# A decoder step on one core: for token blocks 2 and 3 of the last stage, first expert's weighted rows and residual computed on Pool instead of VectorE

## The reference

```python
combine = jnp.sum(jax.nn.one_hot(expert, N_EXPERTS) * w_top[..., None], axis=1)   # two weights per token
for g in range(N_GROUPS):
    act = jax.nn.silu(a) * u * combine[:, sl, None]
    out = out + jnp.einsum('nef,efd->nd', act, w_ed[sl])
x = x + moe(...)                      # the residual
y = _rmsnorm(x, norm_final)           # x * rsqrt(mean(x * x) + 1e-6) * g, the output
```

## Time and profile before

| what | us |
|---|---|
| median of 3 runs | 789.47 (789.15 to 790.32) |
| the profiled execution | 787.27 |
| its span, first to last instruction | 785.1 |
| outside the span | 2.2 |
| TensorE busy | 727.7 |
| VectorE busy | 345.0 |
| ScalarE busy | 245.2 |
| Pool busy | 87.4 |

### The profile page before, as it was taken

The page is one execution under the profiler, slowest core; times in us unless marked ns, Lnnn a source line. Parts: engine busy times, 40 slices in busy tenths (PEclk is TensorE's granted clock), DMA queues, the critical chain, the costliest instruction groups (busy, mean ns, idle before and its releaser), DMA issues.

```text
span 785.1 us, 12498 instructions
## 1 busy us (share of the span) xinstructions
PE 727.7 (93%) x5154; PEld 537.6 (68%) x5154; DVE 345.0 (44%) x648; ACT 245.2 (31%) x495; POOL 87.4 (11%) x143
## 2 busy tenths in 40 slices
PE   4999999999999999999999999988999987877775
PEld 3898997778999999888999987874444332322221
DVE  6653349654565435444255533581222321111228
ACT  6333474554544442334122223321111111001013
POOL 2404000000000100100000001221131211111100
PEclk9999999999999999999999999999999999999998
DMA  8732111114122630722344469898999999999993
GB/s 318 234 109 63 55 54 54 55 54 108 54 59 84 229 142 28 269 81 81 108 149 148 162 201 387 332 336 321 418 417 417 418 418 418 419 417 418 420 388 155
DMA packets 83368, 176.64 MB, mean 225 GB/s; under 512 B 7919, under 2 KB 42063, under 8 KB 83296
## 3 DMA queue, kind: packets, MB, share of 16 engines
q1 hardware_dynamic: 72736, 148.51, 50.8%
q0 software_dynamic: 10576, 27.33, 9.4%
HBM read 161.68 MB, written 22.68 MB: 235 GB/s over the span
## 4 chain that ended last, share of the span: by engine, by line
PE 70%; SPq 14%; DVE 7%; DMA 4%; issue 3%; ACT 3%; ACTq 0%; POOLq 0%; DVEq 0%
PE bank L810 45%; SPq L587 11%; PE bank L1273 7%; PE bank L1290 4%; SPq L593 3%; DMA expert_down<-in_w_exp_down 2%; DVE w_split L1694 2%; ACT w_split L1362 1%; PE bank L830 1%; PE bank L1240 1%; PE bank L1095 1%; PE bank L1101 1%; DVE s_state L1998 1%; PE bank L1046 1%; PE bank L1056 1%
## 5 line engine op out<-in xcount | busy, mean ns | idle before, releaser
L810 PE MATMUL bank<-hT_split,w_split 128*128 128x272 f32 x1152 | 154.1, 292 | 0.0
L810 PEld LDWEIGHTS bank<-hT_split,w_split 128*128 128x128 f32 x1152 | 147.3, 188 | 2.1 <-issue 0.9
L1273 PE MATMUL bank<-expert_gate_up,gatheredT 128*64 128x512 f32 x512 | 116.5, 602 | 18.2 <-DMA expert_gate_up<-in_w_exp_up 16.0
L810 PE MATMUL bank<-w_split,hT_split 128*128 128x512 f32 (+1 forms) x576 | 130.1, 380 | 0.4 <-DVE w_split L1694 0.4
L810 PEld LDWEIGHTS bank<-w_split,hT_split 128*128 128x128 f32 x576 | 100.1, 188 | 22.9 <-issue 3.3
L1694 DVE TENSOR_TENSOR w_split<-w_raw,w_split 128x2048 fp32r<-128x2048 f32 (+1 forms) x35 | 75.9, 2168 | 83.3 <-ACT w_split L1362 83.3
L1273 PEld LDWEIGHTS bank<-expert_gate_up,gatheredT 128*64 128x64 f32 x512 | 39.6, 138 | 91.3 <-issue 67.0
L1362 ACT ACTIVATE w_split<-w_raw 128x2048 fp32r<-128x2048 f32 (+1 forms) x35 | 63.4, 1812 | 42.0 <-PE bank L810 17.5
L1290 PE MATMUL bank<-expert_down,expert_actT 128*64 128x512 f32 x256 | 58.5, 597 | 12.6 <-DMA expert_down<-in_w_exp_down 7.5
L2273 DVE TENSOR_TENSOR expert_act<-expert_silu,bank 128x256 f32<-128x256 f32 x16 | 6.7, 421 | 116.2 <-ACT expert_silu L1635 116.2
L810 PE MATMUL bank<-gla_outT_split,w_split 128*128 128x272 f32 x384 | 49.4, 288 | 0.0
(11 more groups left out here) (405 smaller groups left out, 862.6 us busy)
## 6 DMA issues: line engine op xcount, KB each, us to landing
expert_gate_up<-in_w_exp_gate SPq DMA_DIRECT2D x64, 512.0 KB, 14.9
expert_gate_up<-in_w_exp_up SPq DMA_DIRECT2D x64, 512.0 KB, 15.4
expert_down<-in_w_exp_down SPq DMA_DIRECT2D x32, 1024.0 KB, 17.5
w_raw<-in_w_in SPq DMA_DIRECT2D x15, 1024.0 KB, 5.9
w_raw<-in_w_in SPq DMA_DIRECT2D x16, 512.0 KB, 4.6
s_state<-in_state_gla POOLq DMA_DIRECT2D x4, 1024.0 KB, 10.3
out_sample_gla_state<-s_state POOLq DMA_DIRECT2D x4, 1024.0 KB, 6.1
w_raw<-in_w_proj_gla SPq DMA_DIRECT2D x8, 512.0 KB, 4.3
```

The source lines that it names most:

```text
L810: ins = mm(out, stat(x, k), mov(y, k), start=first and n == 0 and m == 0, stop=last and n == len(ks) - 1 and m == 2)
L1273: ins = mm(P[2 + u][64 * half:64 * half + 64, :].rearrange("p (m n) -> p m n", m=2), XT[0][:, k, 64 * half:64 * half + 64], WGU[gb][:, k / ...
```

## The change

`first_expert` of blocks 2 and 3 leaves VectorE. Pool does it in two instructions for each block: a product of y1 with w1 (`tensor_scalar`), a wait for it, and a sum with `X2` (`tensor_tensor`), each raising `pool_wrote`. On VectorE, `second_expert` of these blocks waits for `pool_wrote` instead of its own earlier instruction. The order on VectorE is changed too: `banks_sum(1)` now stands ahead of `second_expert(2)`.

```diff
+BY_POOL = (2, 3)
@@ gpsimd
             move_rows(turns, 0, last=True)
+            for bl in BY_POOL:
+                pool.wait_ge(x_in[bl], 16 + 32)
+                y1 = YI[2 * bl][:]
+                pool.tensor_scalar(y1, y1, R1["w1"][:, bl:bl + 1], None, ALU.mult).then_inc(pool_wrote, 1)
+                pool.wait_ge(pool_wrote, 4 + 2 * BY_POOL.index(bl))
+                pool.tensor_tensor(y1, y1, X2[:, bl, :], ALU.add).then_inc(pool_wrote, 1)
             for u in range(2):
                 pool.wait_ge(gathered[u], 16 * turns + 16)
@@ vector, second_expert
-                dve.wait_ge(dve_step, added[bl])
+                if bl in BY_POOL:
+                    dve.wait_ge(pool_wrote, 5 + 2 * BY_POOL.index(bl))
+                else:
+                    dve.wait_ge(dve_step, added[bl])
@@ vector, the order at the end
             banks_sum(0)
-            first_expert(2)
             last_norm(0)
+            banks_sum(1)
             second_expert(2)
-            banks_sum(1)
-            first_expert(3)
             banks_sum(2)
             last_norm(1)
             second_expert(3)
```

## The result

| | before | after |
|---|---|---|
| median of 8 runs | 789.93 (789.15 to 790.99) | 792.11 (789.68 to 793.28) |
| the profiled execution | 787.27 | 790.06 |
| its span | 785.1 | 787.9 |
| Pool busy | 87.4 | 98.9 |

The ratio of the times is 1.0034, 95% interval 1.0021 to 1.0047: the change makes the kernel slower, by 2.7 us in the ratio and 2.2 us in the medians. The forecast was 789.9 in a range of 788.0 to 791.7, so it missed by 2.2 us and just outside the range; as a difference it was +0.4 us.

A forecast was written before the change was run, and what follows sets the result against it. VectorE was taken to set the end. Removals 0 and -1.19 us, order 0, waits +0.6 and +1.0 gave +0.4 us: median from 789.5 to 789.9 us, range 788.0 to 791.7.

The forecast's parts named there:

- What Pool's instructions cost: Pool's new work per block: product 1.05 us (bounds 0.93 to 1.9), sum 2.2 us (0.93 to 2.8), wait between 0.15.
- signs of being wrong: Wrong if Pool's sums take under 1.6 or over 2.6 us, or loads land elsewhere than at 765.7 and 769.3.
- the landings: Second loads of blocks 2 and 3, which Pool's products need, arrive at 765.7 and 769.3 us.
- d0: Wait of `last_norm(0)` on VectorE for Pool's sum of block 2, from 768.55 to 769.15: 0.6 us.
- d1: Wait of `last_norm(1)` on VectorE for Pool's second sum, from 774.02 to 775.0: 1.0 us.
- the walk: Last stage followed instruction by instruction on Pool and VectorE; removals, order and two waits together give +0.4 us.
- rival 4: Pool slower than taken, product 1.9 and sum 2.8 us: waits of 4.5 us, net +3.3, 792.8 us; chance 0.15.
- The removal of block 2's instruction: Taking block 2's instruction at 766.73 off VectorE gains 0: its time turns into idle time before the reciprocal.
- Block 3's: Taking block 3's instruction at 772.09 off VectorE, in the dense part, gains 1.19 us.
- The order: On VectorE, `banks_sum(1)` ahead of `second_expert(2)` swaps two instructions of about the same length and costs 0.
- exclude each other: A two-SBUF-input VectorE instruction and a large Pool instruction shut each other out; hold taken as all left of the latter.
- Rival 5: First use on Pool costs extra, some 6 us for newly loaded code: 792 us or more; chance 0.04.

The follow-up runs named there:

- e1: The changed kernel run again with no edit: 792.29 us, ratio 1.0021 to the kernel before.
- e3: The kernel before plus the same four Pool instructions on rows nobody uses, nothing waiting for them: 792.70 us, ratio 1.0035.
- e6: The changed kernel with only block 3 on Pool, block 2 back on VectorE at its old place: 789.37 us, ratio 1.0005.
- e7: The changed kernel with ScalarE making the products of blocks 2 and 3, Pool only the sums: 789.54 us, ratio 1.0005.
- e9: The kernel before, then five instruction forms on Pool alone: product with a constant 2.79 us, product on 512 columns 1.56, copy 1.04, two-tensor product 1.89.
- e5: The kernel before with the new order alone, everything still on VectorE: 788.37 us, ratio 0.9994.
- e4: The kernel before, then Pool's instructions alone and under rows of VectorE instructions; alone product 2.84 us, sum 2.34; whole time not compared.
- e2: The changed kernel without Pool's new work, which nobody does, so outputs of blocks 2 and 3 are incomplete: 788.44 us, ratio 0.9980.
- e11: The changed kernel with idle matmuls filling TensorE's three waits of the last pair: 790.59 us, ratio 1.0030 to the kernel before.

## Why the prediction was wrong

Take the tails apart, each by what its VectorE instructions took over their normal time and by what they started late for want of Pool's result:

| kernel | waits of VectorE | less the removal | tail against before |
|---|---|---|---|
| after, half clock in the last pair | 0.54 + 1.26 | 1.08 | +0.72 |
| e1 | 1.19 + 0.85 + 1.52 | 1.08 | +2.50 |
| e3 | 2.09 + 1.38 | 0 | +3.47 |
| e6 | 1.27 | 1.08 | +0.20 |
| e7 | 0.51 + 0.96 | 1.08 | +0.40 |

Every row adds up to within 0.02 us. Nothing else moves this stage in these profiles.

**The step that failed** is "What Pool's instructions cost": the product. I took 1.05 us, near the fill, with 1.9 as the upper bound. It takes 2.85 us, 1.8 more, and outside the bounds. They came from a fill and a one-column copy, which say what it costs to move columns and nothing of what it costs Pool to compute on them; a single-input instruction was taken to be cheaper than the sum, and it is dearer. The Trainium skill, "GPSIMD Engine Reference", section 4.1, calls one-input elementwise work on Pool roughly line-rate. The copy's 1.04 us agrees with it, the product's 2.85 us does not. The prediction's signs of being wrong watched Pool's sums and the landings, which both came as taken; the product's 1.05 us stood only among what a right forecast would show. Why the product is so slow no run shows: e9 rules out the scalar per partition as the cause, and a large fixed cost (1.56 us for half the columns).

**What followed from it** in an execution with the last pair at full clock (e1). Pool has its sum of block 2 ready not at 766.95 but 0.14 us behind the start of `last_norm(0)`. So the first encounter goes the other way round (d0 is 0, not 0.6), the sum ends at 771.9 and not at 769.15, and VectorE must wait for its result, 1.19 us. The next product then meets `second_expert(2)`, 0.85 us. d1 was 1.0 in the walk and is 1.52. The walk had +0.4; it is +2.5. That the tail of the first profile came out at +0.72, near the forecast, was luck. At full clock it went the way of rival 4, Pool slower than taken, which had 0.15, with 1.9 + 2.8 us taken for what is 2.85 + 2.35. Its waits were placed wrongly (2.1 in front of `last_norm(0)`, none there in fact), and its sum of 4.5 compares with 3.56.

**What held.** The removal of block 2's instruction turned into idle time: 1.54 us in front of the reciprocal where 0.35 was the earlier trace rows, 1.5 forecast. Block 3's is worth 1.08 us where 1.19 was taken. The order costs 0 (e5). The sum takes 2.35 us where 2.2 was taken. Pool and VectorE do exclude each other, in both directions, as the earlier trace rows showed for one: e3 and e4. For the sum, the Trainium skill's rule in "SBUF — State Buffer", section "Who interferes with whom", is what the traces show, and also that a VectorE instruction with one SBUF input goes free. For the product it isn't: the prediction took all that is left of a large Pool instruction as its hold, but e4's 0.78 us of 2.84 is far from a hold for the whole length, and the product of 797.45 waited not for one VectorE instruction but for two. The landings came near where they were forecast: block 2's product starts at 766.08 and 765.62 (765.75 forecast), and block 3's rows land 3.72 us (e6) and 3.30 us (e7) behind the start of `banks_sum(0)`, 3.71 forecast. Rival 5 did not come about. Two instructions that the kernel before lacks, and whose name says that they configure Pool, stand in the trace, but 17 us ahead of the new work, in Pool's idle time, and the first product is no longer than the later ones; what they cost there, if anything, is hidden:

```profile
L794 POOLq MODIFY_POOL_CONFIG  x2: 42/42/42, 749.2 to 749.2; - x2
```

**What the prediction didn't have** is the half clock of the last pair. It isn't the change's: e2 and e5 have it without the new work on Pool, e1 has that work and lacks the half clock. It costs 1.7 us in the x16 group. The order-only kernel has it and still the tail of the kernel before, 15.89 us, so by itself it doesn't change the tail. In the changed kernel it hides 1.8 us of the change's price, because it makes VectorE late and hardly the landings: the tail is 16.61 us with it and 18.39 without. By these tails the change costs 0.7 us in such executions and 2.5 in the others; that rests on one profile with it and two without (e1, e11). What sets it off is not shown.

## What to carry to other kernels

Before moving an instruction to Pool, find or measure that very form there. Here they took: product with a scalar 2.85 us, the same as a two-tensor instruction 1.89, sum 2.35, copy 1.04, all 128x1024 float32, where VectorE does product and sum together in 1.28. An instruction that leaves a dense VectorE for Pool gives back its own time once, 1.1 us here, and takes up to 2.1 us from each two-input VectorE instruction that meets it; by these numbers it can pay beside instructions that read PSUM (twelve of them in e4 lost nothing), or where VectorE is idle; no kernel here tried it. When a stage's parts are late by different causes (landings here, TensorE's clock there), a profile of one execution can show the mild case: take a second one before believing the sum.

## What was not expected of the hardware

- On Pool a product with one tensor input (2.85 us) is slower than a sum with two (2.35 us), 2.5 against 2.1 ns a column; a two-tensor product with a broadcast column is faster than both (1.89 us).
- Pool's product keeps a VectorE instruction with two SBUF inputs out for 0.78 to 0.86 us of its 2.85 us (e4, e1, e11). One that came later was not held at all: in the profile after, `second_expert(2)` starts at 773.51, by estimate 1.2 us into the product (which ended at 775.17 and takes 2.84). Pool's sum keeps it out until about 0.2 us before its own end.
- TensorE's clock drops to 0.50 for some 3 us and twice as long at times, at places that differ between executions of the same kernel: the first profile of the changed kernel has it near 528, 667 and 759 us, the second (e1) only near 528 and 667. What sets it off is not shown; idle time of TensorE stands ahead of the stretch of 759, but as much of it stands there in the kernel before, where no drop follows. One such stretch in the last pair made an x16 group 5.35 us long instead of 3.65, and single runs of the kernel before range over 6 us.
